# Two transformer blocks in one program: slots moved by 128 bytes, router logits before the last norm, and three changes of order

## The chip, the cores and the metric

One core of a Trainium2 chip runs the whole program. The metric is the device time of one execution in microseconds (us). The core has a tensor engine (PE), a vector engine (DVE, VectorE), a scalar engine (ACT, ScalarE), a pool engine (POOL, GpSimd) and a sync engine (SP), each with an instruction stream of its own. ACT, POOL and SP also issue transfers, each in its own queue. PE reads SBUF, the on-chip memory of 128 partitions, and writes PSUM, eight banks of 2 KB per partition.

## The reference

256 tokens of width 1024 in float32 pass through two blocks. All of it, cut to what matters here:

```python
def rms_norm(x, g):
    y = x * rsqrt(mean(x * x, axis=-1) + NORM_EPS)
    return y * g

# block 1: h = rmsnorm(x, ln1_g); z = h @ w_in  (1024 x 8968)
#   sliding-window attention, gated convolution (input columns ub), forgetting attention, block attention
#   x = x + (gated sum of the four branches) @ w_out;   x = x + conv-gated FFN(rmsnorm(x, ln2_g));  rmsnorm(x, final_g)
# block 2:
x = x + concatenate([y_pool, y_diff]) @ w_out
x = x + cross_attention(rms_norm(x, xattn_norm_g), rms_norm(mem, mem_norm_g), w_cq, w_ckv, w_co)
x = x + moe_ffn(rms_norm(x, ffn_norm_g), w_router, b_router, w_gu, b_gu, w_down, b_down)
return rms_norm(x, final_norm_g)

def moe_ffn(h, ...):                      # 32 experts, 4 of them for each token
    logits = h @ w_router + b_router
    top_val, top_idx = top_k(logits, 4);  gates = softmax(top_val)
    # of each expert e, for its tokens: clamped_swiglu(h[tok] @ w_gu[e] + b_gu[e]) @ w_down[e] + b_down[e], times the gate
```

An expert has 8 MB of `w_gu` and 4 MB of `w_down`.

## The kernel before

The five instruction streams are written by hand, one function each: `tensor_program`, `sync_program`, `gpsimd_program`, `scalar_program`, `vector_program`. Each engine counts its finished steps in a semaphore of its own. `Done.step` names a count, and another engine waits for a name (`q.wait_ge(*dve["residual", w, i])`). The order on an engine is the order in which its function issues.

Weights come in units of 1 MB. Each unit goes to one of 15 slots of 2048 float32 per partition (`ring0` to `ring3`, `high0` to `high2`, `h_hi`, `late4`, `late5`, `memx`, `memn`, `memt`, `last0`, `last1`), most of which become free only as the program goes on. `load` (L1297) in `sync_program` takes the slot that has been idle longest, waits until PE has used what it held, and issues the transfer in SP's queue. In the columns of SBUF the areas follow each other: constants, `cols_sb`, x, h, the rounded halves of h, the ring and high slots, and, from a fixed column on, the area of the late, mem and last slots.

Up to the experts the products are made from rounded halves: ScalarE writes the high part of a unit (`high`, L1535), VectorE the rest (`rest`, L1972), in halves of 1024 columns, and `thrice` (L604) issues three matmuls for each product. `ahead` makes the parts of the units that come next. Tokens are the 256 columns of x and h, held as 8 tiles k of 128 channels. The experts' weights are used as they land.

The first unit is `ub` 0, loaded by two transfers of 512 KB: one for each group of 128 columns, all 1024 rows. ScalarE waits for the whole unit, makes its two high parts, then issues the second group of the small vectors (`load_rows(1)`, L1593) and rounds `wfc`, and only then makes the high parts of the next unit.

The relative position bias goes through DRAM: VectorE writes diagonals to `diag_sb`, POOL's queue stores them 23 times over to `diag_dram` (two transfers, L1363) and loads `toep` from there (eight transfers, L1398).

`add_residual(w, norm)` occurs three times, with w = `out` (block 1), `out2` and `co` (block 2). PE makes four groups of two column tiles. VectorE adds each to x (step `residual`), and ScalarE and VectorE write its squares over h. With i = 2 and 3 VectorE also makes the rest parts of the unit of that number. POOL adds squares (L1421), PE sums them over the channels with a matmul against ones, ScalarE takes the root, VectorE the reciprocal (L2014), and `apply` multiplies x by it and by the gain into h. After `co` the router follows: eight matmuls of h with `wrt`, four for each of two sets of rows; ScalarE copies the rows (`logit rows`); PE turns them to tokens and adds the sets (`logits turned`); VectorE adds the bias and picks the four largest (`mask`). PE turns h and x to token rows (L1060; bank results `h_tok`, `x_tok`), counts, and `pick` multiplies a selection matrix with the token rows to gather an expert's tokens. From there on the experts run one after the other (`gate_up`, `down`, `scatter`).

`Banks` deals out the eight PSUM banks in order: a product takes the bank that has been free longest, after the step that read it last.

## Time and profile before

| what | value |
|---|---|
| median of 3 runs | 1724.79 us (1724.74 to 1726.17) |
| the profiled execution, whole | 1726.6 us |
| its span | 1724.8 us |
| PE busy | 1578.4 us (92%) |
| DVE, ACT, POOL busy | 753.1, 482.6, 182.2 us |
| bytes moved | 527.89 MB |

The span is from the first to the last instruction of the trace. A row of the timeline gives the start, the duration, the engine, the line of the helper that issued it, output and inputs, and in brackets how long the engine stood idle before it and what released it. Since helpers issue most instructions, the names of the tiles tell the place.

### The profile page before, as it was taken

What the parts mean: (1) busy time and instruction counts of PE and PEld (TensorE: products, weight loads), DVE (VectorE), ACT (ScalarE), POOL (GpSimd) and SP (SyncE); (2) the same over time, 40 slices, a digit from 0 to 9 for tenths busy, and PEclk for the clock granted to TensorE, in tenths of its full rate; (3) what the DMA queues carried; (4) which work ended last, traced back from release to release, by engine and by line L of the source; (5) the groups of instructions that cost most, each with busy time, mean ns of one, the idle gap of its engine ahead of it and who ended that gap; (6) DMA issues with size and microseconds to landing.
All of it is one profiled execution on the core that took longest, in us unless ns stands there. A gap on an engine that the chain in (4) does not pass through costs nothing.

```text
span 1724.8 us, 22680 instructions
## 1 busy us (share of the span) xinstructions
PE 1578.4 (92%) x9684; PEld 998.8 (58%) x9684; DVE 753.1 (44%) x1333; ACT 482.6 (28%) x825; POOL 182.2 (11%) x208
## 2 busy tenths in 40 slices
PE   7999999999999999989999988888898888889886
PEld 6998899999999989973333322223232322323221
DVE  6798777979884788551221211111121212111121
ACT  4245666455553564530110101010010101001001
POOL 0201102515530041020000000000000000000000
PEclk9999999999999999999999999999999999999999
DMA  9866455556655635658999999999999999999996
GB/s 219 173 206 167 120 135 175 165 171 192 178 194 174 197 117 189 247 199 331 422 421 422 421 421 421 420 421 421 421 421 421 421 422 422 420 421 421 422 421 270
DMA packets 195002, 527.89 MB, mean 306 GB/s; under 512 B 18546, under 2 KB 136351, under 8 KB 145743
## 3 DMA queue, kind: packets, MB, share of 16 engines
q1 hardware_dynamic: 191008, 519.23, 78.8%
q0 software_dynamic: 3344, 6.93, 2.6%
q8 instruction: 78, 1.28, 0.3%
q10 hardware_dynamic: 542, 0.21, 0.1%
q14 instruction: 30, 0.24, 0.0%
HBM read 524.70 MB, written 1.62 MB: 305 GB/s over the span
## 4 chain that ended last, share of the span: by engine, by line
DMA 45%; PE 44%; DVE 7%; ACT 2%; issue 1%; SPq 0%; ACTq 0%; DVEq 0%
PE bank L604 43%; DMA slot_ring<-in_w_down 15%; DMA slot_late<-in_w_down 8%; DMA slot_high<-in_w_down 8%; DMA slot_memx<-in_w_down 8%; DVE slot_ring_r L1972 2%; DMA slot_ring<-in_w_gu 2%; DMA slot_memt<-in_w_gu 2%; DMA slot_ring<-in_w_in 2%; ACT high_r L1535 1%; DVE h_sb L1980 1%; DVE conv L1980 0%; DVE rstd L2014 0%; DVE stat L2190 0%; DVE stat L2408 0%
## 5 line engine op out<-in xcount | busy, mean ns | idle before, releaser
L604 PE MATMUL bank<-h_hi_r,high_r 128*128 128x256 f32 x1000 | 286.7, 287 | 7.7 <-DVE slot_ring_r L1972 3.4
L1972 DVE TENSOR_TENSOR slot_ring_r<-slot_ring,high_r 128x1024 fp32r<-128x1024 f32 x198 | 250.3, 1306 | 78.1 <-ACT high_r L1535 75.8
L604 PE MATMUL bank<-h_lo_r,high_r 128*128 128x256 f32 x1000 | 283.1, 283 | 0.0
L1976 DVE TENSOR_SCALAR ga<-bank 128x512 f32<-128x512 f32 x32 | 22.1, 691 | 591.1 <-PE bank L604 591.1
L604 PE MATMUL bank<-h_hi_r,slot_ring_r 128*128 128x256 f32 x952 | 269.5, 283 | 0.0
L1535 ACT ACTIVATE high_r<-slot_ring 128x1024 fp32r<-128x1024 f32 x198 | 198.0, 1051 | 64.2 <-PE bank L604 43.4
L604 PEld LDWEIGHTS bank<-h_hi_r,high_r 128*128 128x128 f32 x1000 | 191.3, 191 | 11.3 <-DVE h_lo_r L1972 4.3
L1535 ACT ACTIVATE th_e<-ga 128x512 f32<-128x512 f32 x32 | 20.2, 630 | 624.0 <-DVE ga L1976 624.0
L604 PEld LDWEIGHTS bank<-h_lo_r,high_r 128*128 128x128 f32 x1000 | 191.4, 191 | 0.1
L604 PEld LDWEIGHTS bank<-h_hi_r,slot_ring_r 128*128 128x128 f32 x952 | 182.2, 191 | 0.0
L604 PE MATMUL bank<-slot_ring,xg 128*64 128x512 f32 x528 | 124.6, 603 | 11.4 <-DMA slot_ring<-in_w_gu 11.4
L604 PE MATMUL bank<-slot_high,xg 128*64 128x512 f32 x400 | 93.9, 600 | 9.3 <-DMA slot_high<-in_w_gu 9.3
L1524 POOL CAST bias_of_r<-owners_r 128x128 fp32r<-128x128 f32 x32 | 9.3, 293 | 842.0 <-PE bank L604 842.0
L604 PE MATMUL bank<-slot_ring,hbT 128*64 128x512 f32 x304 | 73.3, 602 | 16.9 <-DMA slot_ring<-in_w_down 16.9
L604 PEld LDWEIGHTS bank<-slot_ring,xg 128*64 128x64 f32 x528 | 34.3, 137 | 88.2 <-issue 50.1
L1976 DVE TENSOR_SCALAR seT_r<-bank,const_sb 128x256 fp32r<-128x256 f32 x32 | 15.5, 484 | 154.2 <-PE bank L604 154.2
L604 PE MATMUL bank<-slot_last,xg 128*64 128x512 f32 x304 | 71.3, 599 | 6.1 <-DMA slot_last<-in_w_gu 6.0
L604 PE MATMUL bank<-slot_late,xg 128*64 128x512 f32 x256 | 61.5, 601 | 6.9 <-DMA slot_late<-in_w_gu 6.9
L1535 ACT ACTIVATE hbT<-bank 128x512 f32<-128x512 f32 x32 | 19.1, 597 | 172.0 <-PE bank L1151 171.9
L604 PEld LDWEIGHTS bank<-slot_high,xg 128*64 128x64 f32 x400 | 26.0, 136 | 67.9 <-issue 37.5
L604 PEld LDWEIGHTS bank<-slot_ring,hbT 128*64 128x64 f32 x304 | 19.9, 136 | 68.6 <-issue 39.5
L604 PE MATMUL bank<-slot_high,hbT 128*64 128x512 f32 x200 | 48.2, 602 | 11.1 <-DMA slot_high<-in_w_down 11.1
(441 smaller groups left out, 2901.0 us busy)
## 6 DMA issues: line engine op xcount, KB each, us to landing
slot_ring<-in_w_gu SPq DMA_DIRECT2D x66, 1024.0 KB, 27.0
slot_high<-in_w_gu SPq DMA_DIRECT2D x50, 1024.0 KB, 26.7
slot_ring<-in_w_down SPq DMA_DIRECT2D x49, 1024.0 KB, 26.6
slot_last<-in_w_gu SPq DMA_DIRECT2D x38, 1024.0 KB, 27.1
slot_ring<-in_w_in SPq DMA_DIRECT2D x36, 1024.0 KB, 5.3
slot_late<-in_w_gu SPq DMA_DIRECT2D x32, 1024.0 KB, 26.7
slot_high<-in_w_down SPq DMA_DIRECT2D x25, 1024.0 KB, 27.0
slot_ring<-in_w_up SPq DMA_DIRECT2D x44, 512.0 KB, 4.8
```

Of the source, the lines that this page charges most:

```text
L604: return e.matmul(o, lhs, rhs, start=start, stop=stop, skip_group_check=True)
L1524: e.tensor_copy(bias_of[n % 2].rearrange("p (c s) -> p c s", c=2), owners[:, :, n:n + 1].broadcast_to([P, 2, CAP])).then_inc(*pool.step("b ...
L1535: return e.activation(o, i, f, **k)
L1972: return e.tensor_tensor(o, i, j, op)
L1976: return e.tensor_scalar(o, i, s1, None, op1)
L1980: return e.scalar_tensor_tensor(out=o, in0=i, scalar=s, in1=j, op0=op1, op1=op2)
```

## The change

1. The constants get 96 unused columns at their end, and `COLS` lies 96 instead of 64 floats behind them. All areas from `cols_sb` to the end of the high slots move up by 32 floats, which is 128 bytes. That is 7 of the 15 slots (ring and high) and `h_hi`, which lies among the halves of h; the late, mem and last slots stay. In bytes modulo 256, ring and high slots began at 128 and now begin at 0; `h_hi` began at 32 and now at 160; the others stay at 128.
2. `ub` 0 comes as four transfers of 256 KB, rows 0 to 511 of both column groups first, with a semaphore for these two. `load_rows(1)` and `wfc` come after the high parts of the next units.
3. The diagonals are stored from ScalarE's queue, behind its reads of the products `qa`.
4. In `add_residual` VectorE makes the rest parts of unit 3 after the loop, with those of unit 2 among them (`ahead` makes what is not made yet).
5. The last norm is no longer applied ahead of the router. `wrt` is multiplied by the gains earlier, and the logits are products of x, four of them ahead of the last group of `co`. ScalarE writes h as x times the gain. The factor of each token, from matmuls of the squares (now in `sq_last`) against one column of ones, is applied where the rows of tokens are read from their banks. The turns of x go by column halves, and those of the second half wait for reads of VectorE that come after the mask.

The start on ScalarE's stream, from its first high part on; `high_r<-slot_ring` is a high part, `rows_sb` the small vectors. Before:

```order
L1535 ACTIVATE high_r<-slot_ring_223 128x1024
L1535 ACTIVATE h_hi_r<-h_sb 128x256 x4
L1593 DMA rows_sb<-in_ffn_conv_w 44x128 x2
L1593 DMA rows_sb<-in_attn_norm_g 8x128
L1593 DMA rows_sb<-in_xattn_norm_g 8x128
L1593 DMA rows_sb<-in_mem_norm_g 8x128
L1593 DMA rows_sb<-in_ffn_norm_g 8x128
L1535 ACTIVATE wfc_hi<-wfc 128x64
L1535 ACTIVATE high_r<-slot_ring_224 128x1024 x2
L1535 ACTIVATE high_r<-slot_ring_225 128x1024 x2
```

After:

```order
L1571 ACTIVATE high_r<-slot_ring_224 128x1024
L1571 ACTIVATE h_hi_r<-h_sb 128x256 x4
L1571 ACTIVATE high_r<-slot_ring_225 128x1024 x2
L1571 ACTIVATE high_r<-slot_ring_226 128x1024 x2
L1629 DMA rows_sb<-in_ffn_conv_w 44x128 x2
L1629 DMA rows_sb<-in_attn_norm_g 8x128
L1629 DMA rows_sb<-in_xattn_norm_g 8x128
L1629 DMA rows_sb<-in_mem_norm_g 8x128
L1629 DMA rows_sb<-in_ffn_norm_g 8x128
L1571 ACTIVATE wfc_hi<-wfc 128x64
```

The four high parts of the next two units have moved ahead of the six transfers and of `wfc`.

The end of the residual of `out2` on VectorE; `x_sb<-bank,x_sb` is a residual, `slot_..._r` a rest part. Before:

```order
L1980 SCALAR_TENSOR_TENSOR h_sb<-x_sb 128x512
L1972 TENSOR_TENSOR slot_ring_r<-slot_ring_226,high_r 128x1024 x2
L1980 SCALAR_TENSOR_TENSOR x_sb<-x_sb,cols_sb,rstd 128x256 x2
L1972 TENSOR_TENSOR x_sb<-bank,x_sb 128x512
L1972 TENSOR_TENSOR slot_late_r<-slot_late_227,high_r 128x1024 x2
L2014 RECIPROCAL rstd<-rstd 128x256
```

After:

```order
L2027 SCALAR_TENSOR_TENSOR h_sb<-x_sb 128x512
L2027 SCALAR_TENSOR_TENSOR x_sb<-x_sb,cols_sb,rstd 128x256 x2
L2019 TENSOR_TENSOR x_sb<-bank,x_sb 128x512
L2019 TENSOR_TENSOR slot_ring_r<-slot_ring_227,high_r 128x1024 x2
L2019 TENSOR_TENSOR slot_late_r<-slot_late_228,high_r 128x1024 x2
L2061 RECIPROCAL rstd<-rstd 128x256
```

The rest part of the ring slot has moved behind the last residual.

The router on PE; `mix_hi_r,slot_late_r` are the last products of `co`, `wrt` the router's weights. Before:

```order
L604 MATMUL bank<-mix_hi_r,slot_late_r 128x256
L604 MATMUL bank<-h_sb,const_sb 128x256 x4
L604 MATMUL bank<-h_sb,wrt 32x256 x8
L1060 MATMUL bank<-const_sb,h_sb 128x128 x4
L604 MATMUL bank<-const_sb,mean 128x32 x2
L1060 MATMUL bank<-const_sb,h_sb 128x128 x12
L1060 MATMUL bank<-const_sb,x_sb 128x128 x16
L604 MATMUL bank<-mask,const_sb 128x32 x5
```

After:

```order
L618 MATMUL bank<-mix_hi_r,slot_late_r 128x256
L1081 MATMUL bank<-const_sb,h_sb 128x128 x8
L618 MATMUL bank<-const_sb,sq_last 128x1 x4
L618 MATMUL bank<-x_sb,wrt 32x256 x4
L618 MATMUL bank<-const_sb,sq_last 128x1 x4
L618 MATMUL bank<-const_sb,mean 128x32 x2
L1081 MATMUL bank<-const_sb,h_sb 128x128 x8
L1081 MATMUL bank<-const_sb,x_sb 128x128 x16
L618 MATMUL bank<-mask,const_sb 128x32 x5
```

Half of the logits have moved 48 matmuls up, out of this piece, and eight turns of h stand ahead of the others.

The diff, cut to its core:

```diff
+    parts["unused"] = np.zeros((P, -(sum(a.shape[1] for a in parts.values()) - 3) % P))
-        CONST, COLS = 0, -(-n_const // 8) * 8 + 64
+        CONST, COLS = 0, -(-n_const // 8) * 8 + 96
...
+            unit(name, [(lambda s, j=j, r=r: s.rearrange("p (k n) -> p k n", k=KT)[:, 4 * r:4 * r + 4, j * P:(j + 1) * P],
+                         w[r * 512:(r + 1) * 512, c:c + P].rearrange("(k p) n -> p k n", p=P))
+                        for r in range(2) for j, c in enumerate((c0, c1))])
...
-            add_residual("co", mix_s, lambda k: dve["co split", k // 2], "ffn_g")
+            def logits(ks):
+                q.wait_ge(*dve["router gains"])
+                for k in ks:
+                    q.wait_ge(*dve["residual", "co", k // 2])
+                    m = matmul(bank("router")[k % 4 * NE:(k % 4 + 1) * NE, 0:S], wrt[:, k, :], x[:, k, :], k < 4, k >= 4)
+                return m
...
+            for i in range(3):
+                co_unit(i)
+            banks.take(q, "router")
+            logits(range(0, 4))
+            co_unit(3)
+            turn_h(0)
+            token_squares(0)
+            logits(range(4, KT)).then_inc(*pe.step("router"))
+            token_squares(3).then_inc(*pe.step("sums", "ffn_g"))
...
-            for i in range(2):
-                q.wait_ge(*dve["diag", i])
-                e.dma_start(diag_dram[i * SWA_H:(i + 1) * SWA_H, :, :],
...
-            q.wait_ge(*landed(("ub", 0)))
+            q.wait_ge(*early_in["early"])
             high(("ub", 0), 0)
...
+            q.wait_ge(*landed(("ub", 0)))
             high(("ub", 0), 1)
             round_h("ln1_g", range(KT // 2, KT))
-            load_rows(1)
-            q.wait_ge(*wfc_in["wfc"])
-            af(wfc_s.hi, wfc, ACT.Copy).then_inc(*act.step("wfc hi"))
...
                 evac(("qa", i), qa[:, 2 * i:2 * i + 2, :], two_of(("qa", i)), ("qa", i), HD ** -0.5)
+            for i in range(2):
+                q.wait_ge(*dve["diag", i])
+                e.dma_start(diag_dram[i * SWA_H:(i + 1) * SWA_H, :, :],
...
-            root("ffn_g", EPS2, "xattn_g")
+            evac(("logit rows",), mean_sb, bank("router")[:, 0:S], ("router",))
+            af(token_norm, bank(("ffn_g", "sums"))[:, 0:TT], ACT.Sqrt, bias=eps_col[EPS2]).then_inc(*act.step("root", "ffn_g"))
...
-                    if i >= 2:
-                        ahead((w, i))
+                ahead((w, 3))
...
-            apply("ffn_g", x, h)
...
-            tt(logit, bank("router")[:, S:S + TT * NE].rearrange("p (t n) -> p t n", t=TT),
-               brt.rearrange("p (o n) -> p o n", o=1).broadcast_to([P, TT, NE]), ALU.add).then_inc(*dve.step("logits"))
+                stt(logit[:, t, :], bank("router")[:, S + t * NE:S + (t + 1) * NE], token_norm[:, t:t + 1], brt, ALU.mult,
+                    ALU.add).then_inc(*dve.step("logits"))
```

## Rows read from the trace of the kernel before

**Rows 1.** The page: shares of the chain that ended last, by engine.

```profile
DMA 45%; PE 44%; DVE 7%; ACT 2%; issue 1%; SPq 0%; ACTq 0%; DVEq 0%
```

**Rows 2.** The chain of waits: start, length, what it was.

```profile
922.34 26.91 DMA slot_memx<-in_w_down
...
1698.76 1.96 PE bank L604 x8
```

**Rows 3.** Stretches: length, busy (count) of PE, PEld, DVE, ACT, POOL, PEclk, DMA share, GB/s.

```profile
17.00:22.00 5.00, 4.94 (x22) 4.94 (x23) 4.63 (x11) 2.65 (x6) 0.00 (x0) 1.00 1.20 292
95.00:110.00 15.00, 15.00 (x129) 15.00 (x128) 15.00 (x26) 6.95 (x8) 1.04 (x1) 1.00 0.66 212
677.00:682.00 5.00, 4.57 (x22) 4.28 (x23) 3.64 (x3) 2.65 (x4) 1.13 (x3) 0.66 0.77 229
760.00:770.00 10.00, 8.94 (x62) 6.54 (x62) 6.79 (x26) 5.60 (x10) 1.04 (x3) 0.84 1.00 388
770.00:803.00 33.00, 31.67 (x135) 13.50 (x137) 8.76 (x25) 4.55 (x9) 0.59 (x2) 0.90 0.67 256
803.00:1690.00 887.00, 788.89 (x3603) 268.61 (x3601) 147.39 (x255) 74.16 (x118) 8.71 (x29) 1.00 1.01 420
```

**Rows 4.** DMA issues from 3.1 to 4.0 us: count, KB each, us to landing.

```profile
slot_ring<-in_w_in SPq DMA_DIRECT2D x1, 512.0 KB, 8.3
...
slot_ring<-in_w_in SPq DMA_DIRECT2D x1, 512.0 KB, 9.5
```

**Rows 5.** The timeline at the start.

```profile
13.29 1.06 ACT L1535 ACTIVATE high_r<-slot_ring 128x1024 fp32r<-128x1024 f32 x1 [1.87 <-DMA slot_ring<-in_w_in]
...
27.40 0.36 PE L604 MATMUL bank<-h_hi_r,high_r 128*128 128x256 f32 x1 [1.45 <-DVE slot_ring_r L1972]
```

**Rows 6.** DMA issues of diagonals and the unit behind, and the timeline where it is used.

```profile
diag_dram<-diag POOLq DMA_DIRECT2D x2, 276.0 KB, 12.0
...
slot_ring<-in_w_in SPq DMA_DIRECT2D x1, 1024.0 KB, 17.0
...
87.96 0.39 PE L604 MATMUL bank<-h_hi_r,high_r 128*128 128x256 f32 x1 [1.94 <-DVE slot_ring_r L1972]
```

**Rows 7.** VectorE's timeline behind the last residual of `out`.

```profile
362.81 2.36 DVE L1972 TENSOR_TENSOR slot_ring_r<-slot_ring,high_r 128x1024 fp32r<-128x1024 f32 x2 [1.64 <-ACT high_r L1535]
```

**Rows 8.** VectorE's and then PE's timeline at the last residual of `out2`.

```profile
671.77 3.44 DVE L1972 TENSOR_TENSOR slot_ring_r<-slot_ring,high_r 128x1024 fp32r<-128x1024 f32 x2
...
676.03 0.69 DVE L1972 TENSOR_TENSOR x_sb<-bank,x_sb 128x512 f32<-128x512 f32 x1
...
677.43 0.85 PE L604 MATMUL bank<-h_sb,const_sb 128*128 128x256 f32 x2 [2.06 <-ACT h_sb L1535]
```

**Rows 9.** The timeline from the last residual to the first pick: DVE, ACT, PE.

```profile
754.78 0.69 DVE L1972 TENSOR_TENSOR x_sb<-bank,x_sb 128x512 f32<-128x512 f32 x1 [4.29 <-PE bank L604]
...
767.44 1.28 DVE L1972 TENSOR_TENSOR h_tok_lo_r<-bank,h_tok_hi_r 128x512 fp32r<-128x512 f32 x2
...
763.79 0.38 ACT L1535 ACTIVATE mean<-bank 128x256 f32<-128x256 f32 x1 [5.96 <-PE bank L604]
...
760.28 1.33 PE L604 MATMUL bank<-h_sb,wrt 128*32 128x256 f32 x4 [2.96 <-DVE h_sb L1980]
...
766.80 1.15 PE L1060 MATMUL bank<-const_sb,x_sb 128*128 128x128 f32 x9
768.27 1.27 PE L604 MATMUL bank<-mask,const_sb 128*128 128x32 f32 x10 [0.32 <-DVE h_tok_lo_r L1972]
770.97 0.47 PE L604 MATMUL bank<-sel_r,h_tok_hi_r 128*128 128x256 f32 x2 [1.43 <-DVE cnt L2555]
```

**Rows 10.** GB/s in 40 equal slices of 95 to 110 us.

```profile
GB/s 93 229 341 388 366 385 390 388 232 16 0 0 0 0 22 96 208 325 366 385 390 382 385 230 8 0 0 0 44 0 87 134 292 358 382 390 382 388 322 55
```

**Rows 11.** DMA issues from 880 to 1700 us: count, KB each, us to landing.

```profile
slot_high<-in_w_gu SPq DMA_DIRECT2D x42, 1024.0 KB, 27.0
...
slot_h_hi<-in_w_gu SPq DMA_DIRECT2D x16, 1024.0 KB, 27.3
```

More of the change, by code:

```diff
@@ L408, in hybrid_moe_program @@
         cq, co = memt, mix
+        sq_last = tiles(at("sq_last", AR + TT * D, KT * S), KT)
         es = [at(f"es{i}", GATE + i * 512, 512) for i in range(2)]
@@ L1043, in tensor_program, with co_unit, token_squares @@
             pe.mark("ffn start")
-            add_residual("co", mix_s, lambda k: dve["co split", k // 2], "ffn_g")
-            pe.mark("moe")
-            banks.take(q, "router")
-            b = bank("router")
-            q.wait_ge(*wrt_in["wrt"])
-            for k in range(KT):
-                q.wait_ge(*dve["h", "ffn_g", k])
-                m = matmul(b[k % 4 * NE:(k % 4 + 1) * NE, 0:S], wrt[:, k, :], h[:, k, :], k < 4, k >= 4)
-            m.then_inc(*pe.step("router"))
-            banks.give("router", (dve, "logits"))
+            def co_unit(i):
+                project(("co", i), mix_s, lambda k: dve["co split", k // 2], (dve, ("residual", "co", i)))
+            def logits(ks):
[4 more added lines that the diff above has]
+                return m
+            def token_squares(i):
+                q.wait_ge(*sq_by("ffn_g", i)["square", "ffn_g", i])
+                q.wait_ge(*pool["squares", "ffn_g"])
+                for t in range(TT):
+                    for k in (2 * i, 2 * i + 1):
+                        m = matmul(bank(("ffn_g", "sums"))[:, t:t + 1], sq_last[:, k, t * P:(t + 1) * P], ones[:, 0:1],
+                                   k == 0 and t == 0, k == KT - 1)
+                return m
             def turn_back(name, src, t, c, *until):
@@ L1295, in load @@
                 slot_of[name] = slot
-                for view, src in transfers:
-                    e.dma_start(view(slot_f[slot]), src).then_inc(*slot_in[slot].step("unit", name))
+                for i, (view, src) in enumerate(transfers):
+                    if name == ("ub", 0) and i < 2:
+                        e.dma_start(view(slot_f[slot]), src).then_inc(*early_in.step("early"))
+                    else:
+                        e.dma_start(view(slot_f[slot]), src).then_inc(*slot_in[slot].step("unit", name))
                 idle.append((slot, (used_by, name if isinstance(name, tuple) else (name,))))
@@ L1620, in scalar_program @@
                 ahead(name)
+                if c == 0:
+                    load_rows(1)
+                    q.wait_ge(*wfc_in["wfc"])
+                    af(wfc_s.hi, wfc, ACT.Copy).then_inc(*act.step("wfc hi"))
                 q.wait_ge(*pe[name])
@@ L1750, in add_residual @@
                     if i % 2:
-                        squares(norm, h, x, i, dve["residual", w, i])
+                        squares(norm, squares_of(norm), x, i, dve["residual", w, i])
+                    if norm == "ffn_g":
+                        q.wait_ge(*dve["residual", w, i])
+                        for k in (2 * i, 2 * i + 1):
+                            af(h[:, k, :], x[:, k, :], ACT.Copy, scale=col("ffn_g", k)).then_inc(*act.step("gained", k))
                 ahead((w, 3))
@@ L2293, in add_residual @@
                     if i % 2 == 0:
-                        squares(norm, h, x, i, dve["residual", w, i])
-                    if i >= 2:
-                        ahead((w, i))
+                        squares(norm, squares_of(norm), x, i, dve["residual", w, i])
+                ahead((w, 3))
             dve.mark("ln2 start")
@@ L2346, in vector_program @@
                 if i == 2:
+                    q.wait_ge(*wrt_in["wrt"])
+                    gains = cols_sb[:, col_at["ffn_g"]:col_at["ffn_g"] + KT].rearrange("p (k o) -> p k o", o=1)
+                    tt(wrt, wrt, gains.broadcast_to([P, KT, NE]), ALU.mult).then_inc(*dve.step("router gains"))
                     c1 = 6.28125
```

54 lines of the change are left out of this document (35 added, 19 removed).

## Prediction

> **What bounds the kernel now.** I read three views in order. First the page's line on the chain that ended last: 45% of it is DMA and 44% PE [rows 1]. Then the chain itself, in order of time: up to 922.34 it goes nearly always through PE, from there on through transfers of expert weights of some 27 to 30 us each, until the last one lands and PE goes on at 1698.76 [rows 2]. Then the stretches: from 803 to 1690 us the DMA engines are busy all the time (share 1.01) at 420 GB/s, while PE is busy 789 of 887 us; from 770 to 803 the share is only 0.67 [rows 3]. So there are two parts. Ahead of about 800 us PE sets the pace, since a load waits until PE has used its slot. Behind it the weights arrive at one rate, whatever PE does. A microsecond taken from PE's path ahead of 800 starts the saturated stream a microsecond sooner and moves the end by one. Behind 803 only the rate counts, and 1% of it is 887 / 100 = 8.9 us. The sum is made on the span of the profiled execution, 1724.8 us, which is also the median of the runs (1724.79); the whole execution took 1726.6, so 1.8 us lie around the span, and I add nothing for them.
>
> **The start (parts of `ub` 0, small vectors moved).** Now the two transfers land 8.3 and 9.5 us after issues at 3.2 and 3.7 us, so at 11.5 and 13.3 [rows 4], and ScalarE's first high part starts at 13.29, at once behind the second [rows 5]. After, it waits for the first 512 KB of the unit alone, which should be there when the first transfer landed: 11.5. That is 13.3 - 11.5 = 1.8 us. The second unit's high parts stood behind six small transfers and `wfc`; PE stood idle 1.45 us for the rest part made from them, at 27.40 [rows 5]. With the move that gap is covered. Together 3.3 us. PE does only 22 matmuls in the 5 us from 17 to 22, and 129 in 15 us (43 in 5) later, though the granted clock reads 1.00 in both [rows 3]. If that slow phase ends at the same moment as before, half of the 1.8 us is lost again, and 2.4 are left. I take the middle, **-2.8**, and keep -1.5 (the small vectors now land late and PE waits for them once) and -3.3 as ends.
>
> **The diagonals.** The two stores take 12.0 us for 276 KB each, and the 1 MB unit behind them took 17.0 us; PE stood idle 1.94 us for its rest part at 87.96 [rows 6]. From ScalarE's queue the stores are issued about 3 us later, but POOL's small loads no longer queue behind them. The unit needs to land 2 us sooner out of 17. I take the whole stall, **-1.9**; the other end is 0, if what is slow is not the queue. For ScalarE the two issues cost nothing: it has nothing to do there that PE waits for soon. The first use of the bias is far behind. Row and rule meet here: 276 KB took 12.0 us, where a unit of 1 MB takes 17.0 even in the crowd. The Trainium skill, DMA: Bandwidth & Descriptors, section Rules for kernel authors, says that an outermost dimension smaller than 16 keeps a transfer on at most so many engines, and this one has 8 heads outermost. By that rule the store stays as slow in another queue, the gain is nearer 0, and the sum would be 1.9 us higher.
>
> **The order of rest parts, three times.** Behind `out`: the last residual was released by PE, so it doesn't come sooner. Before, its rest parts ended at 362.81 + 2.36 = 365.17, and the reciprocal follows at once [rows 7]. After, four parts of 2.36 / 2 = 1.18 us stand between the residual (ends at 361.2) and the reciprocal: 361.2 + 4.7 = 365.9. That is a loss of **+0.7**. Behind `out2`: the residual at 676.03 had stood behind two rest parts of 3.44 us, and PE stood idle 2.06 us until it had the squares at 677.43 [rows 8]. Now the residual follows PE. Of 2.06 us some handoff stays: **-1.6**. What comes next on PE is a product of the memory, which doesn't need these rest parts. The stretch 677 to 682 has a granted clock of 0.66, which is 3.4 us at the half level (1.2 GHz) [rows 3], so 1.7 us more could be had if a shorter idle time leaves the clock alone; ends -1.1 and -3.3. Behind `co` the order is part of the next item.
>
> **The last norm.** Before: residual 754.78 (0.69 us), then squares, root, reciprocal and h; the logits at 760.28 (four take 1.33 us); rows copied at 763.79; the two low parts of h, right behind the mask, at 767.44; the count at 768.27; the first pick at 770.97 [rows 9]. After: four logits ahead of the last group of `co` push the residual to the right by 0.85 us, so it ends at 755.5 + 0.85 = 756.3. The squares aren't waited for by the logits: the other four end at 756.4 + 1.3 = 757.7, and the rows are copied at 757.9. From there to the end of the mask it took 767.4 - 763.8 = 3.6 us, and 0.3 more for two additions in place of one: 761.8. Then VectorE makes two low parts of h (1.28 us [rows 9]): 763.2 with the handoff. Here is the new wait: the turns of x of the second half need the banks that these low parts free. Eight turns at 0.13 us (nine took 1.15 [rows 9]): 764.3. From the count to the pick 770.97 - 768.27 = 2.7: 767.0. So **-4.0**. Bounds: the granted clock of 760 to 770 is 0.84, 3.2 us at the half level, which costs 1.6 [rows 3]. It may fall once more in the new idle time (-2.4) or not at all (-5.6). The multiplication of `wrt` by the gains is one VectorE instruction much earlier, where PE is the bound for hundreds of microseconds: nothing. ScalarE's eight products with the gain lie beside PE's last group of `co`, but for the last two, which end with the last logits: nothing.
>
> **The slots moved by 128 bytes.** No row shows a slot at the new residue, so the price is bounded. From above: rows of 1 KB reach at most 390 GB/s [rows 10], rows of 8 KB 420. On one of 16 engines that is 42 ns for 1 KB and 311 ns for 8 KB, so some 3.5 ns of each row, 1.1%, don't grow with its size; a better start can't take more away. For 7 of 15 slots: 0.011 x 7/15 x 887 = 4.6 us. From the other side: loads to `h_hi`, which begins at another residue, land in 27.3 us, to the high slots in 27.0 [rows 11], again 1.1%, so up to +4.6. I take **0**: two residues that differ in the trace differ by 0.3 us in 27, in the direction that would not reward a change, and the stretch runs at the engines' limit.
>
> **Sum.** -2.8 - 1.9 + 0.7 - 1.6 - 4.0 = -9.6; 1724.8 - 9.6 = **1715.2 us**. The clock's phases ahead of 800 us (0.84, 0.90, 0.66 [rows 3]) can shift with any of this, by some 2 us either way: 1712 to 1719 is the forecast's own range.
>
> **Rivals.** First: the aligned slots do load faster. Against it stands the row on `h_hi`; for it, that no row shows an aligned start. Price -4.6: 1710.6 us. The Trainium skill, DMA: Bandwidth & Descriptors, section How a descriptor splits into AXI transactions, states that a descriptor that doesn't start on 256 bytes has its first transaction start at the boundary below and pays for the unused bytes. By its beats of 32 bytes a row of 8 KB at 128 costs 260 instead of 256, an estimate of 1.5% x 7/15 x 887 = 6.3 us. By that rule `h_hi` (1 beat) should have beaten the high slots (4 beats); the trace doesn't agree, it has 27.3 against 27.0.
>
> Second: the router's gain is eaten by its new wait. The turns of x wait for VectorE, PE idles in the middle, and the clock falls over the first picks as it did from 770 to 803 (0.90). The pick comes at 771 as before: 1715.2 + 4.0 = 1719.2. For it: PE's idle times at this place are short and many, and VectorE was the last releaser at 768.27 and 770.97 [rows 9].
>
> Third, the change doesn't do what it says: the unit behind the diagonals is as late as before (+1.9), the first half lands no sooner than the whole, since the four transfers share the engines (+1.8), and the clock takes 2 us: 1715.2 + 5.7 = 1720.9, with the ends of the residuals up to 1723. I set 1722.
>
> Fourth, slower: the moved slots are written at a lower rate. At 8.9 us for each 1% of the whole rate, it takes 9.6 + 3.4 = 13 us, 1.5%, to end slower than before, so a rate under 414 GB/s. At 2% it is 1715.2 + 17.8 = 1733. For it speaks only that 7 slots now have the same residue with nothing in the trace to compare; against it, that 1.5% over all needs 3% on the moved slots, three times what residues differ by in [rows 11].
>
> **Chances.** Forecast 0.60; faster slots 0.13; the router's wait 0.12; the third 0.09; slower 0.06. A measurement of this kernel can tell about 0.2%, 3.4 us, from no change, so below 1721.3 is faster: 0.60 + 0.13 + 0.12 = 0.85; within 0.2% 0.09; slower 0.06. The range takes in the first three with their clock phases: 1706 (both the aligned slots and the good ends of the clock) to 1721.
>
> **What would show it.** First high part at 11.5; no gap of PE over 1 us at the second unit of `ub`, and none at 86. Last residual of `out2` at 674, PE on its squares at 675.5. From the last residual of `co` to the first pick 11.4 us (755.6 to 767.0) instead of 16.2. From the first pick on the same length as before to the end, 420 GB/s in the saturated stretch, and the ring and high slots landing in 27 us. A rate of 424 or more, or of 416 or less, would make the term of the alignment wrong; it is the one that could outweigh all others. The forecast is also wrong if the sum of PE's gains ahead of the experts isn't found again in the time of the first load that saturates.

## The result, and the profile after

The changed kernel takes 1707.39 us (median of 4 runs, 1704.1 to 1708.08) against 1725.48 before; the ratio is 0.9886, with a 95% interval of 0.9864 to 0.9908. That is some 18 us less where 9.6 were forecast. Its profiled execution took 1708.08 us, its span is 1706.3, against 1724.8.

| stretch of the profiled execution (its end before, after) | before | after | difference | forecast |
|---|---|---|---|---|
| to PE's first product of the first unit (17.06, 18.87) | 17.1 | 18.9 | +1.8 | -1.8 |
| to the first scores (140.80, 138.94) | 123.7 | 120.1 | -3.7 | -2.9 |
| to PE's products behind `out` (370.73, 368.50) | 229.9 | 229.6 | -0.4 | +0.7 |
| to the mixing of block 2 (637.02, 634.61) | 266.3 | 266.1 | -0.2 | 0 |
| to PE's products of the cross attention (709.08, 703.57) | 72.1 | 69.0 | -3.1 | -1.6 |
| to the first pick (770.97, 761.36) | 61.9 | 57.8 | -4.1 | -4.0 |
| to the end of the span | 953.8 | 944.9 | -8.9 | 0 |

Up to the first pick the sum is -9.6, by accident just the forecast; behind it, from there to the end of the span, another 8.9 us are gone. The ends of the stretches are rows of the chain of waits (start, length, what) of before

```profile
140.80 0.63 DVE score_swa L1972 x2
...
370.73 197.10 PE bank L604 x1639
...
637.02 13.73 PE bank L604 x80
...
709.08 9.47 PE bank L604 x64
```

and of after, whose further rows answer to [rows 2]:

```profile
3.76 11.33 DMA slot_ring<-in_w_in
15.11 1.07 ACT high_r L1571
...
138.94 0.63 DVE score_swa L2019 x2
...
368.50 197.03 PE bank L618 x1639
...
634.61 1.74 PE bank L618 x8
...
703.57 9.41 PE bank L618 x64
...
943.60 26.08 DMA slot_ring<-in_w_down
...
1680.38 1.96 PE bank L618 x8
```

The page's shares of the chain that ended last, after, answer to [rows 1]:

```profile
PE 49%; DMA 40%; DVE 7%; ACT 2%; issue 1%; SPq 0%; POOL 0%; DVEq 0%; ACTq 0%
```

DMA takes over at 943.60 instead of 922.34, has 40% of the chain for 45%, and its pieces take 25.7 to 28.8 us where they took 26.9 to 30.8. The stretches of after (columns as in [rows 3]):

```profile
634.00:638.00 4.00, 3.91 (x22) 3.58 (x23) 4.00 (x4) 3.82 (x11) 0.00 (x0) 1.00 0.11 24
672.00:682.00 10.00, 9.28 (x68) 8.39 (x68) 9.96 (x18) 4.80 (x10) 1.62 (x4) 1.00 0.67 210
...
803.00:1690.00 887.00, 794.74 (x3630) 270.55 (x3626) 149.41 (x257) 76.89 (x122) 8.79 (x29) 1.00 1.01 425
```

The saturated stretch moves 425 GB/s where it moved 420 [rows 3]: 1.2% more, with the share at 1.01 as before. The granted clock behind the squares of `out2` is 1.00 where it was 0.66 [rows 3], and at the mixing ahead of it, from 634 on, also 1.00. Of before, there:

```profile
636.00:640.00 4.00, 3.50 (x11) 2.91 (x12) 4.00 (x6) 2.61 (x6) 0.00 (x0) 0.61 0.00 0
```

**The start** came out the wrong way. The chain's row at 3.76 is the second early transfer of the first unit, which landed at 15.09 us, not at 11.5. The issues from 3.85 to 7.6 us (count, KB each, us to landing) show what is new there:

```profile
slot_ring<-in_w_in SPq DMA_DIRECT2D x3, 256.0 KB, 11.3
...
wrt<-in_w_router POOLq DMA_DIRECT2D x1, 128.0 KB, 8.5
pos_i<-in_positions POOLq DMA_DIRECT2D x1, 128.0 KB, 8.4
lams<-in_lambda_q POOLq DMA_DIRECT2D x2, 32.0 KB, 5.8
lams<-in_lambda_k POOLq DMA_DIRECT2D x2, 32.0 KB, 6.7
```

With `brt` these are seven small loads in POOL's queue. Before, they stood behind POOL's wait for the diagonals and were issued from 59.8 us on:

```profile
wrt<-in_w_router POOLq DMA_DIRECT2D x1, 128.0 KB, 15.5
pos_i<-in_positions POOLq DMA_DIRECT2D x1, 128.0 KB, 14.9
lams<-in_lambda_q POOLq DMA_DIRECT2D x2, 32.0 KB, 12.1
lams<-in_lambda_k POOLq DMA_DIRECT2D x2, 32.0 KB, 12.9
```

The timeline of ScalarE and PE after (it answers to [rows 5]): the first high part waits 4.01 us and PE stands idle 4.90 us, but no idle time stands at the second unit any more.

```profile
15.11 1.06 ACT L1571 ACTIVATE high_r<-slot_ring 128x1024 fp32r<-128x1024 f32 x1 [4.01 <-DMA slot_ring<-in_w_in]
...
18.87 0.55 PE L618 MATMUL bank<-h_hi_r,high_r 128*128 128x256 f32 x1 [4.90 <-DVE h_lo_r L2019]
```

**The diagonals** (issues at 68.61 to 76 us; they answer to [rows 6]): the unit takes 9.0 us to landing in place of 17.0, the loads of `toep` 7.0.

```profile
slot_ring<-in_w_in SPq DMA_DIRECT2D x1, 1024.0 KB, 9.0
...
toep<-diag_dram POOLq DMA_DIRECT2D x8, 128.0 KB, 7.0
```

PE has no idle time in brackets from 72 to 95 us. The trace has no landing for the two stores themselves, but POOL's wait for them:

```profile
71.72 4.79 POOL L1433 DMA_DIRECT2D toep<-diag_dram  x8 [5.62 <-DMA diag_dram<-diag]
```

The second store was issued at about 59.3 us, so it took some 12.4 us in ScalarE's queue too.

**The rest parts.** VectorE behind the last residual of `out` (for [rows 7]) has four parts in a row and the reciprocal behind them; PE at the squares of `out2` (for [rows 8]) waits 0.65 us in place of 2.06.

```profile
357.72 0.69 DVE L2027 SCALAR_TENSOR_TENSOR x_sb<-bank,x_sb 128x512 f32<-128x512 f32 x1 [4.24 <-PE bank L618]
358.32 4.62 DVE L2019 TENSOR_TENSOR slot_ring_r<-slot_ring,high_r 128x1024 fp32r<-128x1024 f32 x4
362.86 1.74 DVE L2061 RECIPROCAL rstd<-rstd 128x256 f32<-128x256 f32 x1
```

```profile
671.71 1.13 PE L618 MATMUL bank<-h_sb,const_sb 128*128 128x256 f32 x4 [0.65 <-ACT h_sb L1571]
...
678.99 0.36 PE L618 MATMUL bank<-h_hi_r,high_r 128*128 128x256 f32 x1 [0.45 <-DVE h_lo_r L2019]
```

At 678.99 PE is through with the product of the memory and waits for the first tile of h, and the next tiles come at 679.63 and 680.36, 0.7 us apart. In that time PE has three matmuls to do, which follow each other at 0.12 us elsewhere. Before, PE came to h later than h was ready.

**The router** (for [rows 9]; DVE, then PE):

```profile
749.91 0.69 DVE L2019 TENSOR_TENSOR x_sb<-bank,x_sb 128x512 f32<-128x512 f32 x1 [5.04 <-PE bank L618]
...
756.36 1.40 DVE L2027 SCALAR_TENSOR_TENSOR h_tok_lo_r<-bank,token_norm,h_tok_hi_r 128x512 fp32r<-128x512 f32 x2
```

```profile
757.25 1.29 PE L1081 MATMUL bank<-const_sb,x_sb 128*128 128x128 f32 x8 [1.91 <-ACT h_tok_hi_r L1571]
...
761.36 0.76 PE L618 MATMUL bank<-sel_r,h_tok_hi_r 128*128 128x256 f32 x2 [1.43 <-DVE cnt L2607]
```

The new wait is there: the second turns of x stand 1.91 us for their banks. The row names ScalarE's part of h, but in the code the two readers of these banks are ScalarE's parts, which had ended at 755.1, and the low parts from 756.36 on. So the wait is VectorE's, and x12 (the last norm alone, below) names it at this place:

```profile
761.03 1.29 PE L1080 MATMUL bank<-const_sb,x_sb 128*128 128x128 f32 x8 [0.24 <-DVE h_tok_lo_r L2023]
```

From the last residual to these turns it takes 7.3 us in both. With the wait, it is 11.4 us from the residual to the pick.

### The profile page after: what moved, and what is told of

Its sections match the earlier page's. It is cut to its first block, busy times and chain, and to the rows that moved or that the text cites. A ratio compares the mean times of both kernels' runs of the same rounds, so it can differ in the third digit from the quotient of the medians.

```text
span 1706.3 us, 22700 instructions
## 1 busy us (share of the span) xinstructions
PE 1572.5 (92%) x9692; PEld 996.9 (58%) x9692; DVE 748.1 (44%) x1327; ACT 486.4 (29%) x833; POOL 179.5 (11%) x206
## 4 chain that ended last, share of the span: by engine, by line
PE 49%; DMA 40%; DVE 7%; ACT 2%; issue 1%; SPq 0%; POOL 0%; DVEq 0%; ACTq 0%
PE bank L618 48%; DMA slot_ring<-in_w_down 16%; DMA slot_high<-in_w_down 8%; DMA slot_late<-in_w_down 8%; DMA slot_memx<-in_w_down 6%; DVE slot_ring_r L2019 2%; DMA slot_ring<-in_w_gu 2%; DMA slot_ring<-in_w_in 1%; ACT high_r L1571 1%; DVE h_sb L2027 1%; DVE conv L2027 0%; DVE rot_tmp L2499 0%; DVE rstd L2061 0%; DVE stat L2237 0%; DVE stat L2457 0%
```

## The experiments

Every kernel is compared with the kernel before on the same chip; "rate" is that of the stretch 850 to 1650 us, "pick to end" the time from the first pick to the end of the span. The last two begin where the changes of order end; x12, x14 and x15, which change order alone, leave the pick to end at before's 953.8.

| kernel | us (median) | ratio, interval | rate, GB/s | pick to end |
|---|---|---|---|---|
| before | 1725.5 | 1 | 421 | 953.8 |
| changed | 1707.4 | 0.9886, 0.9864 to 0.9908 | 426 | 944.9 |
| x1 slots moved alone | 1715.2 | 0.9929, 0.9908 to 0.9951 | 426 | 943.8 |
| x2 longer constants alone | 1724.4 | 0.9991, 0.9979 to 1.0002 | 421 | 954.5 |
| x3 changed, all 14 slots | 1706.3 | 0.9888, 0.9864 to 0.9913 | 427 | 943.1 |
| x4 changed, slots back | 1718.1 | 0.9956, 0.9939 to 0.9973 | 421 | 953.9 |
| x5 late slots alone | 1714.4 | 0.9945, 0.9928 to 0.9961 | 426 | 942.3 |
| x6 ring slots, areas not | 1714.9 | 0.9941, 0.9924 to 0.9957 | 426 | 944.9 |
| x7 areas, no slot | 1723.1 | 0.9981, 0.9971 to 0.9992 | 421 | 952.9 |
| x9 three slots | 1721.0 | 0.9969, 0.9955 to 0.9983 | 423 | 948.9 |
| x10 all at 32 | 1728.7 | 1.0023, 1.0006 to 1.0039 | 420 | 954.7 |
| x11 all at 192 | 1727.7 | 1.0004, 0.9988 to 1.0019 | 421 | 954.4 |
| x12 last norm alone | 1720.5 | 0.9968, 0.9953 to 0.9983 | 421 | 953.8 |
| x13 diagonals alone | 1727.4 | 1.0006, 0.9994 to 1.0019 | 421 | 955.3 |
| x14 rest parts alone | 1729.0 | 1.0015, 1.0000 to 1.0031 | 421 | 953.8 |
| x15 start alone | 1721.1 | 0.9976, 0.9964 to 0.9989 | 421 | 953.8 |
| x8 changed, small loads later | 1703.8 | 0.9875, 0.9858 to 0.9891 | 426 | 944.2 |
| x16 together | 1702.1 | 0.9866, 0.9845 to 0.9887 | 427 | 942.9 |

### What raised the rate: the slots or the inputs

The change does two things that could: it moves slots, and it makes the rows of the constants longer, behind which the weights may lie elsewhere in DRAM.

x1:

```diff
-        CONST, COLS = 0, -(-n_const // 8) * 8 + 64
+        CONST, COLS = 0, -(-n_const // 8) * 8 + 96
```

> The kernel before with one edit: the 7 ring and high slots, h, x and the columns lie 128 bytes further on, nothing else. The changed kernel moved 425 GB/s in the stretch 803 to 1690 us, the kernel before 420, and from the first pick to the end it took 944.9 us instead of 953.8. Theory A (the start of the moved slots modulo 256 bytes sets the rate): 425 GB/s here too, 8 to 9 us less from the first pick to the end, about 1716 us in all. Theory B (the rate comes from something else in the change, such as the longer rows of the constants, which may shift where the weights lie in DRAM): 420 to 421 GB/s and 1725 us.

x2:

```diff
+    parts["unused"] = np.zeros((P, -(sum(a.shape[1] for a in parts.values()) - 3) % P))
```

> The kernel before with the 96 unused columns of the constants only; no slot moves. Theory A (slots): 420 to 421 GB/s in the saturated stretch and 1725 us. Theory B (where the inputs lie in DRAM): 425 GB/s and about 1716 us.

x4, the changed kernel with

```diff
-        CONST, COLS = 0, -(-n_const // 8) * 8 + 96
+        CONST, COLS = 0, -(-n_const // 8) * 8 + 64
```

> The changed kernel with its 7 slots back where they were, 128 modulo 256 bytes, with the longer constants kept. Theory A: 420 to 421 GB/s, 1716 us. Theory B: 425 GB/s, 1707 us.

Theory A holds on all three in the rate and in the pick to end; the whole of x4 is 2 us above the 1716 that were expected. The stretch from 850 to 1650 us of before (columns as in [rows 3]):

```profile
850.00:1650.00 800.00, 708.01 (x3234) 240.99 (x3236) 132.81 (x231) 66.86 (x108) 8.41 (x28) 1.00 1.01 421
```

The same of x1:

```profile
850.00:1650.00 800.00, 716.65 (x3280) 244.51 (x3276) 135.88 (x235) 69.14 (x110) 8.41 (x28) 1.00 1.01 426
```

x1 alone brought 0.71%, some 12 us by its ratio and 10 by pick to end; x4 put the rate back to 421 and the pick to end back to 953.9, which is before's.

### How it depends on which slots are moved

x3, the changed kernel with

```diff
-        AREAS = 53184 - AR
+        AREAS = 53152 - AR
```

> The changed kernel with its late, mem and last slots moved 128 bytes down too, so that 14 of 15 slots begin at 0 modulo 256 bytes (h_hi stays at 160). Theory A: the other 7 slots give as much again, 429 to 430 GB/s, and the whole takes 1707 - 9 = 1698 us. Theory B: no more than the changed kernel, 425 GB/s and 1707 us.

x5, the kernel before with the same line, so only late, mem and last slots:

> The kernel before, with its other seven slots moved (late, mem, last: 128 bytes down, to 0 modulo 256) and the ring and high slots left at 128. Moving the ring and high slots alone had brought 426 GB/s from 421 in the stretch 850 to 1650 us, and moving the other seven as well 427. Theory A1 (the start of some slots is what counts, and the loss of one slot is hidden or paid by the whole stream): about as much from this half, 425 to 426 GB/s and 1716 us. Theory A2 (what counts is that the ring slots, or something that moved with them, lie right): 421 GB/s and 1725 us.

x6, the kernel before with

```diff
-        CONST, COLS = 0, -(-n_const // 8) * 8 + 64
+        CONST, COLS = 0, -(-n_const // 8) * 8 + 32
...
-        AR = HIGH0 + HIGHS * SLOT
+        AR = HIGH0 + HIGHS * SLOT + 32
```

> The kernel before with the ring and high slots at 0 modulo 256 bytes (reached from below, 128 bytes down, so 256 modulo 512), and with the areas behind them, where the experts' tables and hidden rows lie, left where they were. Theory A1: 426 GB/s, 1715 us. Theory A3 (the areas behind the slots count, not the slots): 421 GB/s, 1725 us. If the residue modulo 512 counts rather than 256: 421 GB/s too.

x7, the kernel before with the second of these lines only:

> The kernel before with only the areas behind the slots moved by 128 bytes (token rows, tables, hidden rows), no slot. Theory A1: 421 GB/s, 1725 us. Theory A3: 426 GB/s, 1715 us.

x9, the kernel before with

```diff
-        HIGH0 = RING0 + RING * SLOT
+        HIGH0 = RING0 + RING * SLOT + 32
```

> The kernel before with only the three high slots moved to 0 modulo 256 bytes (the areas behind them move along, which had done nothing by themselves). Each half of the slots (7 of 15) had brought all of the gain, 426 GB/s from 421 in the stretch 850 to 1650 us. Theory S (one aligned slot now and then lets the stream catch up): 425 to 426 GB/s here too. Theory T (the gain grows with the share and is merely full at a half): 3 of 15 bring half of it, 423 GB/s.

Theory A's first form, each moved slot pays for itself, fell with x3: the other seven gave 1 GB/s where 4 to 5 were expected, and no time that the runs can tell (1706.3 and 1707.4). But x5 shows that those seven bring the whole gain if they are the ones at 0 and the others are not. The stretch of x5:

```profile
850.00:1650.00 800.00, 714.35 (x3261) 242.71 (x3263) 133.28 (x231) 67.23 (x107) 8.12 (x27) 1.00 1.01 426
```

The stretch of x3:

```profile
850.00:1650.00 800.00, 714.33 (x3261) 242.13 (x3259) 131.94 (x228) 66.61 (x106) 8.12 (x27) 1.00 1.01 427
```

The stretch of x7:

```profile
850.00:1650.00 800.00, 708.54 (x3238) 241.21 (x3236) 133.30 (x231) 67.26 (x107) 8.47 (x28) 1.00 1.01 421
```

The stretch of x9:

```profile
850.00:1650.00 800.00, 711.41 (x3251) 242.53 (x3252) 133.61 (x232) 67.61 (x108) 8.46 (x28) 1.00 1.01 423
```

None of 15 slots at 0: 421. Three: 423. Seven, whichever: 426. Fourteen: 427. x6 has the ring and high slots 256 bytes below where x1 has them, so at the other residue modulo 512, and gains the same: 256 is what counts. In x7 the areas behind the slots moved alone, and the rate stayed at 421. In x9 the gain can be seen to come in stretches. All 15 slots are loaded once in some 37 us, and the three high slots and `h_hi` come one behind the other. Its stretches of 5 us:

```profile
1025.00:1030.00 5.00, 3.99 (x18) 0.97 (x16) 0.00 (x0) 0.00 (x0) 0.00 (x0) 1.00 1.01 421
1030.00:1035.00 5.00, 3.87 (x16) 0.97 (x16) 0.00 (x0) 0.00 (x0) 0.00 (x0) 1.00 1.02 424
1035.00:1040.00 5.00, 3.95 (x17) 1.11 (x18) 2.43 (x4) 0.66 (x2) 0.00 (x0) 1.00 1.02 428
1040.00:1045.00 5.00, 5.00 (x26) 2.17 (x26) 0.99 (x2) 1.26 (x2) 0.30 (x1) 1.00 1.02 429
```

428 and 429 GB/s in ten of the 37 us, 416 to 426 in the others of this turn. One turn proves little, since slices of 5 us scatter from 413 to 428 in the kernel before too. But over the 22 turns from 840 us on, the two slices of 4 us from 24 to 32 us behind the first issue to the high slots, which is when these loads come in, average 426 and 427 GB/s, and the other slices 421 to 424. In the kernel before all of them average 420 to 422. That is what theory T expects. Why it is full at half the slots isn't settled: in x1 the unmoved slots stand in short runs among moved ones, in x9 in a run of twelve, so the length of the run may count as well as the share. No run tells these two apart.

### Which starts are good

x10 (residue 32) and x11 (residue 192), the kernel before with

```diff
-        CONST, COLS = 0, -(-n_const // 8) * 8 + 64
+        CONST, COLS = 0, -(-n_const // 8) * 8 + 40
...
-        AREAS = 53184 - AR
+        AREAS = 53160 - AR
```

and with 80 and 53200.

> The kernel before with 14 slots beginning at 32 modulo 256 bytes in place of 128 (h_hi at 192). If the cost is the unused bytes from the boundary below up to the start, 32 costs a quarter of what 128 costs: 425 GB/s (126 bytes of 8 KB against 421 for 128). If it is one more piece for each row, whatever the distance: 421 GB/s as before.

> The kernel before with 14 slots beginning at 192 modulo 256 bytes in place of 128 (h_hi at 96). If the unused bytes below the start count, 192 costs half as much again as 128: 418 to 419 GB/s, some 1729 us. If one more piece for each row counts: 421 GB/s, 1725 us.

The rates are 420 and 421; the stretch of x10:

```profile
850.00:1650.00 800.00, 704.69 (x3216) 238.88 (x3216) 132.59 (x229) 67.21 (x107) 8.42 (x28) 1.00 1.01 420
```

So 32, 128 and 192 cost about the same, and of the four starts tried only 0 is better. How far a row of 8 KB begins from a boundary of 256 bytes didn't matter in these three; that it doesn't begin on one did. The Trainium skill, DMA: Bandwidth & Descriptors, section How a descriptor splits into AXI transactions, has both in it: the first transaction starts at the boundary below, and the unused bytes cost beats. Worked out from that, as an estimate, such a row takes 33 transactions in place of 32, and 257, 260 or 262 beats in place of 256 for a start at 32, 128 or 192. The runs agree with the count of transactions in that all three starts cost alike, and speak against the beats: by these, 32 would have been 1.2% faster than 128, and it was 0.2% slower. In size they confirm neither: one transaction in 32 would be 3.1%, and from none to 14 slots at 0 the rate rose by 1.4% (421 to 427). The page speaks of bytes fetched, while here only the destination moved. Why the extra costs what it costs stays open.

### The start and the diagonals

x8, the changed kernel with

```diff
+            q.wait_ge(*pe[("ub", 1)])
             for i, n in enumerate(("lambda_q1_2", "lambda_k1_2", "lambda_q2_2", "lambda_k2_2")):
```

> The changed kernel, with one wait: POOL issues its seven small loads (lambdas, router weights, positions) after the second unit's products. With the diagonals' stores gone from POOL's queue these loads are issued at 3.9 to 7.5 us, where they stood behind the stores at 59.8 to 63.4 before, and the second early part of the first unit lands at 15.1 us, where 11.5 was forecast. Theory P (the small loads delay it): it lands at 11 to 12 us, PE's first product is 3 to 4 us earlier, and the whole takes 1707.4 - 3 = 1704 us. Theory Q (four smaller transfers are slow in themselves): it lands at 14 to 15 as now, and the whole takes 1707 us.

Theory P. ScalarE's timeline in x8:

```profile
11.33 1.05 ACT L1572 ACTIVATE high_r<-slot_ring 128x1024 fp32r<-128x1024 f32 x1
```

And PE's:

```profile
15.10 0.35 PE L618 MATMUL bank<-h_hi_r,high_r 128*128 128x256 f32 x1 [0.78 <-DVE h_lo_r L2020]
```

The high part starts at 11.33, where 11.5 was forecast, and PE 3.8 us earlier than in the changed kernel. The first pick came 4.0 us earlier (757.36), the whole is at 1703.8, 3.6 us below. The two intervals overlap, so it is the profiles, not the time of the whole, that carry this. There the two groups stand apart: the second early transfer lands at 11.0 us in x8 and in x16, which have the wait, and at 14.4, 15.1 and 17.0 in x3, the changed kernel and x4, which don't.

x13, the diagonals alone, the lines that store them moved as in the change:

> The kernel before with the diagonals' two stores moved from POOL's to ScalarE's queue, nothing else. If POOL's seven small loads, now issued at 4 to 8 us, are what delays the start: the second half of the first unit lands 2 to 4 us later than 13.3 us, and the gap of 1.94 us at 86 is gone, together 0 to 2 us slower up to 140 us, whole about 1725. If the queue was the only effect: first half as before, 1.9 us faster, 1723.

ScalarE's timeline in x13:

```profile
18.43 1.06 ACT L1531 ACTIVATE high_r<-slot_ring 128x1024 fp32r<-128x1024 f32 x1 [6.04 <-DMA slot_ring<-in_w_in]
```

The start is 5.1 us later (18.43 for 13.29), more than expected. In eleven profiles whose start is the same program as before, the high part began at 12.8 to 14.5 us, so at least 3.9 us of it is the change's. There is no idle time at 72 to 95 us, and the whole is the same as before (1.0006). So this part by itself moves the crowd from 60 to 80 us, where it cost 1.9, to the first 18 us, where it costs 4 to 5. The stores stayed at some 12 us in ScalarE's queue, so the queue was not what made them slow. In the changed kernel the unit behind them landed in 9.0 us all the same. In every such kernel the seven small loads were gone from beside it as well; no run moves these loads and leaves the stores in POOL's queue, so which of the two freed the unit isn't shown.

x15, the start alone (the first unit's four transfers, the two waits, the small vectors moved):

> The kernel before with the first unit by parts of its rows and the small vectors behind the next high parts; the diagonals stay in POOL's queue. If the parts themselves are good and only the small loads spoilt them: first high part at 11 to 11.5 us, no gap at the second unit, PE's 33.4 us mark at 30.6, whole about 1722. If four transfers are slow in themselves: first high part at 14 to 15 us, whole 1725.

ScalarE's timeline in x15:

```profile
12.39 1.06 ACT L1546 ACTIVATE high_r<-slot_ring 128x1024 fp32r<-128x1024 f32 x1 [1.18 <-DMA slot_ring<-in_w_in]
```

First high part at 12.39, 0.9 us earlier instead of 1.8; no idle time at the second unit; first scores at 137.36 us (140.80 before, and 139.1 to 144.9 in the eleven profiles whose start is that of before); ratio 0.9976, some 4 us. The stall of the diagonals is there (1.32 us at 84.38), as expected with the stores in POOL's queue.

### The rest parts and the last norm

x14:

```diff
-                    if i >= 2:
-                        ahead((w, i))
+                ahead((w, 3))
```

> The kernel before with the rest parts of the units 2 and 3 behind the last residual, three times. Forecast's terms: +0.7 behind out, -1.6 behind out2 (-3.3 if the clock's stretch at the half level goes too), after co nothing to split: PE's idle time at the squares of out2 0.6 in place of 2.06 us, whole 1723 to 1724.

PE's timeline in x14, at the squares of `out2`:

```profile
677.24 1.13 PE L604 MATMUL bank<-h_sb,const_sb 128*128 128x256 f32 x4 [0.65 <-ACT h_sb L1535]
```

The idle time is 0.65 us and the granted clock from 677 to 682 us is 1.00. From the first scores to the last residual of `co` it takes 611.2 us (143.37 to 754.57) against 614.0 before (140.80 to 754.78). But the whole did not get faster: 1.0015, 1.0000 to 1.0031. Its own first 140 us, which are the same program as before, came out 2.6 us later, and from the residual to the pick it took 17.1 us instead of 16.2, both inside what kernels with this part unchanged show. The place shows the gain, the clock of the whole doesn't; whether it is real in most runs is open.

x12, the last norm alone (the changed kernel with all else as before; the rest parts in the old order too):

> The kernel before with the last norm of the change alone (logits from x, four ahead of the last group, factor of each token later, turns by halves), nothing else moved. The forecast's term: 4.0 us less from the last residual to the first pick, whole 1725 - 4 = 1721 us, and 421 GB/s in the saturated stretch. If the gain is given back in the first expert: 1725 us.

PE's first pick in x12:

```profile
764.78 0.55 PE L617 MATMUL bank<-sel_r,h_tok_hi_r 128*128 128x256 f32 x1 [1.43 <-DVE cnt L2604]
```

From the last residual (753.70) 11.1 us, for 16.2 before. The twelve profiles with the old router have 16.2 to 17.1 there, and the five others with the new one 11.4 to 12.5. The ratio is 0.9968, some 5.5 us, and nothing is given back: 953.8 us from the pick to the end, as before.

x16, x8 with 53152 for 53184 and, in `add_residual` on VectorE,

```diff
+                    if i >= 2 and w == "out":
+                        ahead((w, i))
```

> The changed kernel with the seven small loads issued after the second unit's products (1703.8 us alone), all 14 slots at 0 modulo 256 bytes (427 in place of 426 GB/s: 1 us) and the old order of the rest parts behind out (0.5 us): 1702.3 us. If the small terms are given back: 1704.

1702.1 us, the lowest of all medians. It can't be told from x8 (1703.8), but is clearly below the kernel before.

**How far to trust one profile.** The first 140 us are the same program in before, x1, x2, x5, x6, x7, x9, x10, x11, x12 and x14, but for addresses. The first scores came at 140.8, 141.1, 139.1, 139.4, 141.8, 142.8, 140.8, 144.9, 144.6, 141.8 and 143.4. So up to 6 us of difference between two profiles ahead of 140 us means nothing by itself. The stall of 1.94 us [rows 6] is missing in x2 and x5, and is 0.8 to 2.9 us in the others. The time of the whole has its own limit: x7, which keeps the rate at 421 and all orders, has a ratio of 0.9981 (0.9971 to 0.9992), so a term of 3 us can't be read from a ratio alone.

## Why the prediction was right or wrong

**The slots: wrong, and the miss of the whole.** The term was 0 with bounds of 4.6 either way; it was -8.9 by the profile (953.8 to 944.9) and -10 to -12 by x1. The forecast's low end, 1706 us, had the slots at -4.6 and the rest from good phases of the clock. Three steps failed.

First, the row on `h_hi` was read as if it compared a good residue with a bad one. Its 32 and the others' 128 are both bad (x10), so 27.3 against 27.0 us said nothing on 0; those times are moreover those of a load with others queued ahead of it (27 us for 1 MB, of which the stream moves one in 2.5), and measure the queue. Second, the bound of 1.1% for a row was near the mark for a row (420 to 425 is 1.2%), but multiplying it by 7/15 was wrong: that each slot pays only for its own loads was assumed, and x5, x6 and x3 show that seven slots bring what fourteen do. Without the factor the bound would have been 9.8 us. It would have held the 8.9 of the changed kernel, but not the 10.0, 10.7 and 11.5 of x1, x3 and x5, so the bound itself was a little small too. Third, the weighing: the rival that came true had been given a chance of 0.13 and about half of its size. The estimate of 1.5% for a row, which the prediction worked out from the Trainium skill (DMA: Bandwidth & Descriptors, How a descriptor splits into AXI transactions), was nearer than the row on `h_hi` that I weighed against it, though x10 and x11 speak against the beats that it came from.

**The start: wrong in sign.** -2.8 was forecast, and the first product came 1.8 us later, and the vanished gap at the second unit gave 1.45 back behind it. The four transfers themselves did as said in x8, where the high part began at 11.33 us for 11.5, and half of it in x15, with 12.39. PE's slow first phase did not end at its old moment, as one end of the term had it: its first 24 products took 5.3 us both before (from 17.06) and after (from 18.87). The step that failed is in the part on the diagonals. It says that POOL's small loads no longer queue behind the stores and stops there. They don't go away; POOL issues them as soon as it can, at 3.9 us, among the loads that PE waits for. x8 prices this at 3.6 to 4.0 us in the changed kernel, x13 at 4 to 5. The third rival had the start late too, because four transfers share the engines; x8 has the same four transfers without the delay.

**The diagonals: right in the term, incomplete as a price.** -1.9, and no idle time is left. Of the twelve profiles with the stores in POOL's queue ten have the stall, of the six with them in ScalarE's none. The reason given, that the small loads no longer stand beside the unit, fits the runs but isn't separated from the move of the stores. The row and the rule that I set against each other were both right: the stores stayed slow, at some 12 us. The Trainium skill (DMA: Bandwidth & Descriptors, Rules for kernel authors) says that an outermost dimension smaller than 16 keeps a transfer on at most so many engines; the trace agrees as far as that 12 us in one queue stayed 12 in the other. The unit came in time nevertheless. The stores were issued at 58.5 us, as before, not 3 us later. In x13, which moves them alone, the start lost 4 to 5 us where the stall had cost 1.9.

**The rest parts.** Behind `out` +0.7 was forecast. The four rest parts run in a row as said, from 358.4 to 362.9, and the reciprocal begins 5.1 us behind the residual's start in place of 4.6: +0.5.

Behind `out2` the term was -1.6 with an end at -3.3 if the clock stays up. The idle time fell by 1.4 (2.06 to 0.65) and the clock was up, but that second gain was not kept: from the squares to the products of the cross attention it takes 31.9 us (671.71 to 703.57) where it took 31.7 (677.43 to 709.08). PE reaches h sooner now, and h isn't there sooner, since four rest parts stand between the residual and the reciprocal. I had looked only at the first product behind the squares, not at where PE meets h again. So the term is -1.4 + 0.2 = -1.2. Nor is the clock behind the squares the new order's alone: x6, x11 and x12 have the old order, the same idle time of 2.07 us, and 1.00 there, while nine others with it read 0.66; all six with the new order read 1.00. The other 1.7 to 1.9 us of the stretch's -3.1 lie ahead of it, where the clock was at 0.61 from 636 to 640 before and at 1.00 after. Of the ten profiles that are the program of before up to there, five have it low at this place (0.57 to 0.62) and five at 1.00 (x2, x6, x7, x11, x12). So it isn't the change's.

**The last norm: right.** -4.0 forecast, -4.1 measured to the first pick: 16.2 to 11.4 us from the last residual, less the 0.6 by which the residual itself comes later behind the products of the cross attention (46.3 us for 45.7), where the four early logits had been put at 0.85. The new wait on the low parts is there, with 1.91 us. The rival that it would eat the gain fell with this and with x12.

**The sum.** -1.9 up to the first scores where -4.7 was forecast, -0.9 between 140 and 245 us where the granted clock was higher (0.97 for 0.95; of the chain's pieces of 118 matmuls the first took 15.3 us for 16.5), +0.5 behind `out`, -0.2 up to the mixing, -3.1 and -4.1 make the -9.6 up to the pick, but for rounding. That this is the forecast's sum is luck: 2.8 us missing at the start, and 2.6 to 2.8 of clock that it had not counted on. The whole was missed by the last row of the table.

## What to carry to other kernels

When a transfer is taken out of a queue, ask not only what no longer waits behind it but when that will now be issued, and who else is loading then. If a transfer-bound stretch writes rows whose starts share a bad residue, try residue 0 modulo 256 bytes on the chip before arguing about its price: it is one constant, and here it was worth at least as much as all changes of order together (x1 has a ratio of 0.9929, x4 of 0.9956). And compare at points that depend on one part only (here the time from the first pick to the end), since the whole, and above all the first 140 us, scatter by more than the small terms.

## What the runs showed of the hardware

- Loads of 8 KB rows into SBUF ran at 420 to 421 GB/s with no start on a 256-byte boundary (before, x2, x4, x7, x10, x11), at 426 with 7 of 15 slots on one (x1, x5, x6) and at 427 with 14 (x3). Starts at 32, 128 and 192 modulo 256 were alike within 1 GB/s.
- The gain isn't in proportion to the share of slots: 3 of 15 gave 2 GB/s (x9), 7 gave 5, 14 gave 6.
- Seven small loads of together 400 KB, issued at 3.9 to 7.5 us, delayed the landing of a 256 KB transfer that was issued at 3.76 us, ahead of them all: 11.0 us without them (x8, x16), 14.4 to 17.0 with them (x3, changed, x4).
- A store of 276 KB with 8 heads outermost took 12.0 us in POOL's queue and some 12.4 in ScalarE's.
- The same program read a granted clock of 0.57 to 0.62 at one place in five profiles and of 1.00 in five others.
